# A hybrid decoder layer on one core: the sample batch's mixing and paged attention laid as strands between half units of the input projection

## The reference

```python
h = rms_norm(x, norm_g)
z = h @ w_in          # 1024 -> 5280 columns: q_r k_r v_r g_r | c_q c_kv k_pe | g_m | mg_r mg_m
# branch A: retention, 4 heads of 128, chunks of 128; rotary q and k, per-head decay, a state per head
ret = head_rms(inner + cross) * silu(g_r)
# branch B: latent attention, 8 heads; q = rms_norm(c_q) @ w_uq; keys and values from rms_norm(c_kv)
mla = softmax(q k^T * 96 ** -0.5) v * silu(g_m)
merged = sigmoid(mg_r) * (ret @ w_branch_ret) + sigmoid(mg_m) * (mla @ w_branch_mla)
y = rms_norm(x + merged @ w_out, final_gain)
```

## Time and profile before

| | |
|---|---|
| median of 3 runs | 2914.07 us (2908.35 to 2914.93) |
| profiled execution | 2911.8 us, span 2909.6 us, mean granted clock 0.926 |
| busy, share of the span | PE 2595.7 us (89%), PEld 2343.4 (81%), DVE 1365.3 (47%), ACT 1083.7 (37%), POOL 541.0 (19%) |
| DMA | 326.22 MB, mean 112 GB/s |

### The profile page before, as it was taken

The page is one execution under the profiler, slowest core; times in us unless marked ns, Lnnn a source line. Parts: engine busy times, 40 slices in busy tenths (PEclk is TensorE's granted clock), DMA queues, the critical chain, the costliest instruction groups (busy, mean ns, idle before and its releaser), DMA issues. The chain is left out here.

```text
span 2909.6 us, 46992 instructions
## 1 busy us (share of the span) xinstructions
PE 2595.7 (89%) x15975; PEld 2343.4 (81%) x15975; DVE 1365.3 (47%) x2631; ACT 1083.7 (37%) x2340; POOL 541.0 (19%) x435
## 2 busy tenths in 40 slices
PE   7899999997899999983479999498989995899998
PEld 6799999996688888862368887487878884799897
DVE  4243334444243344424256664286868884322221
ACT  3122223333122223321157776275757774211110
POOL 0000024331011034421024445000000000223230
PEclk9999999999999999996589997599999997999997
DMA  4354565552345565622244440523232303443440
GB/s 129 111 153 135 143 168 137 136 143 89 108 146 148 148 176 152 158 75 74 82 118 118 122 128 2 130 59 74 59 74 59 74 1 139 151 153 115 144 129 24
DMA packets 422336, 326.22 MB, mean 112 GB/s; under 512 B 81153, under 2 KB 391522, under 8 KB 419042
## 3 DMA queue, kind: packets, MB, share of 16 engines
q1 hardware_dynamic: 405906, 307.72, 38.1%
q10 hardware_dynamic: 16208, 15.74, 1.8%
HBM read 221.92 MB, written 101.43 MB: 111 GB/s over the span
## 5 line engine op out<-in xcount | busy, mean ns | idle before, releaser
L66 PE MATMUL f_bank<-a_h_hi,a_w_hi 128*128 128x384 f32 (+3 forms) x1680 | 609.2, 363 | 15.1 <-DVE a_zo L805 10.2
L68 PE MATMUL f_bank<-a_h_hi,a_w_lo 128*128 128x384 f32 (+3 forms) x1680 | 595.0, 354 | 0.0
L67 PE MATMUL f_bank<-a_h_lo,a_w_hi 128*128 128x384 f32 (+3 forms) x1680 | 594.6, 354 | 0.0
L66 PEld LDWEIGHTS f_bank<-a_h_hi,a_w_hi 128*128 128x128 f32 (+1 forms) x1680 | 315.3, 188 | 42.1 <-issue 15.4
L68 PEld LDWEIGHTS f_bank<-a_h_hi,a_w_lo 128*128 128x128 f32 (+1 forms) x1680 | 314.5, 187 | 30.7
L67 PEld LDWEIGHTS f_bank<-a_h_lo,a_w_hi 128*128 128x128 f32 (+1 forms) x1680 | 315.4, 188 | 26.3
L2343 DVE TENSOR_TENSOR t_pt<-t_bank,t_pt 128x512 fp32r<-128x512 f32 (+3 forms) x320 | 194.7, 609 | 68.7 <-ACT t_pt L2295 66.1
L2295 ACT ACTIVATE t_pt<-t_bank 128x512 fp32r<-128x512 f32 (+3 forms) x320 | 170.9, 535 | 140.4 <-PE t_bank L2428 139.8
L2353 DVE TENSOR_REDUCE t_mx<-t_bank 128x1 f32<-128x512 f32 (+3 forms) x320 | 192.4, 604 | 51.5 <-PE t_bank L2420 42.9
L2308 ACT ACTIVATE t_prob<-t_bank,t_nm 128x512 f32<-128x512 f32 (+3 forms) x320 | 196.7, 626 | 36.3 <-DVE t_nm L2360 35.2
L2439 PE MATMUL t_bank<-t_pt,t_vt 128*128 128x256 f32 x1088 | 192.1, 301 | 7.8 <-DVE t_pt L2343 6.3
(11 more groups left out here) (375 smaller groups left out, 5424.2 us busy)
## 6 DMA issues: line engine op xcount, KB each, us to landing
a_w_raw<-in_w_in SPq DMA_DIRECT2D x82, 512.0 KB, 4.4
p_lat<-in_lat_pool SPq DMA_DIRECT2D x208, 128.0 KB, 2.0
between_zT<-a_zo SPq DMA_DIRECT2D x82, 256.0 KB, 4.5
y_mg<-between_zT SPq DMA_DIRECT2D x128, 128.0 KB, 2.2
between_zT<-a_zo SPq DMA_DIRECT2D x82, 192.0 KB, 2.5
r_zt<-between_zT SPq DMA_DIRECT2D x16, 768.0 KB, 7.3
t_qt<-between_QT SPq DMA_DIRECT2D x16, 768.0 KB, 11.8
a_x<-in_x_prompt SPq DMA_DIRECT2D x16, 512.0 KB, 5.1
```

Of the source, the lines that this page charges most:

```text
L66: pe.matmul(out, lh, rh, start=start, stop=False)
L67: pe.matmul(out, lh, rl, start=False, stop=False)
L68: return pe.matmul(out, ll, rh, start=False, stop=stop)
```

## The change

- `mix` (for the sample rows), `latent_queries`, `attend_paged` and `latent_values` go, with their barriers. Their work becomes strands in `front`: the sample rows are tile -1 of `mla_steps(0, 8)`; then come `decode_steps()` (labels D, V), `sample_ret_steps()` (labels E), `ret_steps(0, 8)`, `mla_steps(8, 16)`, `ret_steps(8, 16)`, one chain of steps spread evenly over all of the projection from half unit 37 on.
- A group of 512 keys goes through in one sweep: each group has its own maximum, its own sum and its own values (`acc`), which `d_join` weighs together at the end of a sequence. The two parts of the rotary keys stand one above the other (64 rows), so that one matmul of 512 columns takes the place of eight of 128; the new keys are one group of 64 columns with a mask. All pages are loaded by SP, three groups ahead.
- Of the wait at a strand's start only SP's is left (and one of POOL's).
- Sigmoid becomes Tanh of half the argument in `front`: silu is (tanh + 1) z, made in `a_zo`, and the factors of 2 go into the head norm's constants and into `w_mla` and `w_out` (0.5). The scale of the scores goes into the norm of c_q; in `attend` one negated maximum replaces a maximum and a multiplication. The rotary turns have other forms of about the same size.
- The x tiles of the first half have a buffer each and are loaded at once.

In the cut below `d_load` and the branches of `which` are SP's, `d_exp` to `d_part` ACT's, the other `d_` functions PE's.

```diff
+def decode_steps():
+    out = [PAD, PAD, ("S", "D", 0), *(("DL", j) for j in range(3)), PAD, PAD, PAD, ("DN", 0), ("DT", 0), PAD]
+    late = []
+    for i in range(N_GROUPS):
+        b, g = divmod(i, PER)
+        for x in (("DS", i), ("DT", i + 1), ("DP", i), ("DO", i)):
+            out.append(x if x[1] < N_GROUPS else PAD)
+            if x[0] == "DS" and i:
+                out.append(("DN", i))
+            if late:
+                out.append(late.pop(0))
+        if g < NGD and b * NGD + g + 3 < DEC_B * NGD:
+            out.append(("DL", b * NGD + g + 3))
+        if g == NGD:
+            late += [("DE", b, k) for k in range(5)] + [("DF", b)]
+    for x in late:
+        out += [x, PAD]
+    return out + [("S", "V", 0), ("VL", 0), PAD, PAD, ("VX", 0), PAD, PAD, ("VP", 0), ("VP", 1), PAD, ("VO", 0)]
+
+def sample_ret_steps():
+    out = [PAD, PAD, ("S", "E", 0), ("EL", 0), PAD, PAD, ("Ef", 0), ("Ev", 0), ("Ef", 1), PAD, ("Eh", 0), ("Ef", 2), PAD, PAD, ("Ek", 0), ("Em", 0),
+           ("Ea", 0), PAD]
+    for h in range(RH):
+        out += [PAD, ("Eo", h), PAD, ("Es", h)]
...
 def schedule():
     (a1, b1, a2, b2), units = backbone()
...
+    first = next(i for i, x in enumerate(a1) if x[0] == "U" and x[2] == 1 and units[x[1]][0] == 6)
+    steps = mla_steps(0, 8) + decode_steps() + sample_ret_steps() + ret_steps(0, 8) + mla_steps(8, 16) + ret_steps(8, 16)
+    return a1[:first] + between(a1[first:] + b1 + a2 + b2, steps), units
...
+            def d_load(j):
+                need(sp, nl, j - 3)
+                need(sp, tq, 3 * (j - 3))
+                for k in range(4):
+                    page = sp.value_load(table[0:1, 4 * j + k:4 * j + k + 1])
+                    sp.dma_start(lat[:, j % 4, k], T["lat_pool"][ds(page, 1)].rearrange("a p c -> (a p) c")).then_inc(lin[j % 4], 16)
+                    sp.dma_start(pe[:, j % 4, k], T["pe_pool"][ds(page, 1)].rearrange("a p c -> (a p) c")).then_inc(lin[j % 4], 16)
...
+                elif which == "D":
+                    mla_over(sp, 8)
...
+                elif which == "E":
+                    sp.wait_ge(v_st, 32)
...
+                elif x[0] == "DT":
+                    if n:
+                        d_exp(n - 1)
+                    d_keys_high(n)
+                elif x[0] == "DS":
+                    d_low(n)
...
+                elif x[0] == "DP":
+                    d_probs_high(n)
+                elif x[0] == "DO":
+                    d_part(n)
...
+            def d_turn(i):
...
+                for c in range(KC):
+                    need(p, ltl, 3 * (j - 1) + c + 1)
+                    for k in range(4):
+                        mm = p.transpose(bk[:, 2 + c, k * PAGE:(k + 1) * PAGE], lat[:, j % 4, k, c * P:(c + 1) * P], ident[:])
+                    mm.then_inc(tq, 1)
+                need(p, ltl, 3 * j)
+                for k in range(4):
+                    mm = p.transpose(bk[0:ROPE, 4, k * PAGE:(k + 1) * PAGE], pe[:, j % 4, k], ident[:])
+                mm.then_inc(tq, 1)
+            def d_scores(i):
...
+                for c in range(KC):
+                    for x in range(2):
+                        p.matmul(bk[:, 5, 0:w], qall[:, c, bb], keys[x][:, c, 0:w], start=(c + x == 0), stop=False)
+                p.matmul(bk[:, 5, 0:w], qp[:, bb], rope[:, 0:w], start=False, stop=True).then_inc(qk, 1)
+            def d_probs(i):
+                bb, g = divmod(i, PER)
+                p.wait_ge(ex, i + 1)
...
+            def d_values(i):
+                bb, g = divmod(i, PER)
+                p.wait_ge(ptl, i + 1)
...
-            a.activation(sg[:, 0:n], bk[:, b, 0:n], ACT.Sigmoid).then_inc(sig, 1)
+            a.activation(zo[:, u % 3, 0:n], bk[:, b, 0:n], ACT.Tanh, scale=0.5).then_inc(sig if kind == "silu" else z_act, 1)
...
-    mix(nc, T, True)
-    decode(nc, T)
```

More of the change, by code:

```diff
@@ L112 @@
          + [(c * P, P, "silu") for c in range(3 * RH, 4 * RH)])
-GATES = [(GM0 + c * P, P, "silu") for c in range(NH * VD // P)] + [(MG0 + c * P, P, "sigmoid") for c in range(2 * D_MODEL // P)]
+GATES = [(GM0 + c * P, P, "silu") for c in range(NH * VD // P)] + [(MG0 + c * P, P, "tanh") for c in range(2 * D_MODEL // P)]
 BLOCKS = [(h, *b) for h in range(2) for b in PLAIN + GATES]
@@ L201, in mla_steps @@
         if n == lo:
-            out.append(("MX", lo, 2))
+            out.append(("MX", lo, "uv"))
         if n + 2 < hi:
@@ L275, in front @@
             event[x[:2]] = len(fate)
-            if BLOCKS[units[x[1]][0]][3] == "sigmoid":
+            if BLOCKS[units[x[1]][0]][3] == "tanh":
                 n_sig += 1
@@ L325, in front @@
                 pass
-            kn_hi, kn_lo = pair(of, "kn", [P, NH // 2, 2 * P])
+            with nc.sbuf_tensor("m_wt", [NOPE, NH, KL], F32) as w_t:
+                pass
+            with ExitStack() as k:
+                kn_hi, kn_lo = (k.enter_context(nc.sbuf_tensor("m_kn" + x, [P, NH // 2, 2 * P], F32R)) for x in ("_hi", "_lo"))
+            of("gap", [P, QC * NH * QD])
+            qall, qp = of("qall", [P, KC, DEC_B, P], F32R), of("qp", [2 * ROPE, DEC_B, P], F32R)
+            ltn = [of("ltn" + x, [P, KC, NS], F32R) for x in ("_hi", "_lo")]
@@ L797, in z_out @@
                 j, g, half_, c0, width, kind, t0, n = unit(u)
-                if kind == "sigmoid":
+                if kind == "tanh":
                     return
@@ new lines, in d_fold, with v_heads @@
+            def d_fold(bb):
+                p.wait_ge(de, 15 * (bb + 1))
+                p.wait_ge(oc, min(PER * (bb + 1) + 1, N_GROUPS))
+                for c in range(KC):
+                    mm = p.matmul(bk[:, 6, c * NS:(c + 1) * NS], tot[:, c * P:(c + 1) * P], fold[:], start=True, stop=True)
+                mm.then_inc(of_d, 1)
+            def v_heads(k):
+                p.wait_ge(v_lo_d, 2)
+                for h in range(4 * k, 4 * k + 4):
+                    f = slice(h // 2 * P, (h // 2 + 1) * P)
+                    for c in range(KC):
+                        mm = three(p, bk[:, 5, h * NS:(h + 1) * NS], uvv_hi[:, c, f], uvv_lo[:, c, f], ol_hi[:, c, h], ol_lo[:, c, h], c == 0, c == KC - 1)
+                if k:
+                    mm.then_inc(v_mm, 1)
@@ new lines, in e_outs @@
+            def e_outs(h):
+                p.wait_ge(e_a, 4)
+                p.wait_ge(e_v, 3)
+                p.wait_ge(e_qm, h + 1)
+                p.wait_ge(e_split, 2 * h + 2)
+                out = bk[0:NS, 6, h * RD:(h + 1) * RD]
+                three(p, out, ea_hi[:, h], ea_lo[:, h], ev_hi[:, h], ev_lo[:, h], True, False)
+                for b in range(DEC_B):
+                    i = three(p, out, qm[0][:, b], qm[1][:, b], es_hi[:, b], es_lo[:, b], False, b == DEC_B - 1)
+                i.then_inc(e_o, 1)
```

1865 lines of the change are left out of this document (721 added, 1144 removed).

## The result

The changed kernel takes 2962.4 us (median of four runs, 2961.4 to 2964.3) against 2914.1 us: ratio 1.016, 95% interval 1.0138 to 1.0183. It is slower by 1.6%; the forecast was 2786 us, 4.4% faster. Its profiled execution has a span of 2959.5 us, 1.9 us under its own time.

What follows compares the result with a forecast made beforehand. PE was nearly gapless in the projection but idle in the stages before `attend`. Span 2909.6 - 538.1 + 293.6 = 2665, + 56 + 78 - 15 = 2784, 2.2 more as a time: 2786 us; range 2690 to 2862.

Steps and rivals of the forecast that it cites:

- the step on the clock: At strand starts in `front`: waits of about 8 us and more cost clock, three new ones at 3.3 us each, 10 us.
- What goes, and the PE work that comes: Four stages and barriers go, 538.1 us; their work returns between half units as 293.6 us of PE time.
- Waits inside a group: In the key groups, mainly the values' product awaiting split probabilities: 0.5 us a group, 32 us, plus 24 at sequence ends, 56.
- Rival 2: Order binds: ACT's queue puts next keys before probabilities; 2 us more a group or SP's pages add 70 us: 2857; chance 0.2.
- SP's pages: SP's page loads take 6 us of a group's 9.2, with stores of z behind them; nothing was taken for it.
- Waits at strand starts: In `front`, a new strand's first step waits for its load; with denser strands and clock, 78 us in sum.
- the second half's x tiles: In the projection, 8 of the 18.4 us of waits for `a_h_lo` were to go, since group steps lie between.
- Rival 3: Slower: two table loads a key group if Exp and Tanh need different tables, 320 us, a time near 3100; chance 0.05.
- The group term's upper bound: In the key groups: 2.5 us a group, 160 us, if every probabilities' turn and values' product waits for its own chain.
- signs that were to prove the forecast wrong: PE waiting over 1.5 us a group, waits for pages or `a_zo`, or table loads beside the gates.
- signs that were to confirm it: `attend` starting near 1718 us; in the paged strand groups 9.8 us apart, PE over 90% busy at full clock.
- rival 1: All group chains hidden, leaving only strand starts: 2665 + 50 - 15, time about 2700; chance 0.2.

Runs made afterwards that it cites:

- e3: On the changed kernel, all steps of the key groups made blank slots, so the paged attention is left out; 2531.5 us.
- e2: On the changed kernel, each key group's values product done one group late, everything computed; 2891.2 us, ratio to the kernel before 0.991.
- e7: On top of e2, no strand's steps beside the 12 half units in which the second half of x is turned; 2877.5 us.
- e4: No part of the block: runs of 512-column matmuls with waits of about 0.5 to 9 us between, single and in trains; no kernel time given.
- e11: e4 again, with waits of about 1.3 to 4.4 us, each six times, behind runs of 90 to 105 matmuls; no kernel time given.
- e14: On the changed kernel, DVE makes the low half of the split probabilities three times over, lengthening each group's chain; 3044.4 us.
- e1: On the changed kernel, the groups' values product reads a static tile, so PE never waits for the split probabilities; output not attention; 2903.1 us.
- e13: On top of e2: e7's cleared half units, blank slots where strands start, two more in each retention tile; 2855.9 us, ratio to the kernel before 0.979.

## Why the prediction was wrong

The mechanism of the waits was seen, their size was not, and the step on the clock failed. The 180 us by which `front` came late are 72 of clock, 64 of idle time and 44 of dearer work.

**What goes, and the PE work that comes.** Right in kind. The groups' turns, keys and values cost more than 3.90 us: by the starts in the changed kernel at full clock DO takes 1.05 us (540.29 to 541.34) and DS 1.46, against 1.01 and 1.14. The fifth product of DS, with 64 rows, was counted at 0.227 and takes 0.43 to the next start. Some 0.3 us x 64 is about 20 us of the miss. The rest is for the most part what a change of kind costs on either side of a step: in a half unit of 384 columns the first product behind a DS, DT or DP takes 0.26 to 0.28 us to the next start in place of 0.173, and the one ahead of a DP 0.27. By an estimate of three such places a group that is another 20 us; where the few us that are left lie is open. The sum priced every product as if its like stood beside it.

```profile
541.34 0.40 PE L1595 MATMUL f_bank<-d_lt_hi,m_qall 128*128 128x512 f32 x1
...
542.37 0.50 PE L1596 MATMUL f_bank<-d_rt,m_qp 64*128 64x512 f32 x1
542.80 0.44 PE L66 MATMUL f_bank<-a_h_hi,a_w_hi 128*128 128x384 f32 x1
543.08 0.34 PE L67 MATMUL f_bank<-a_h_lo,a_w_hi 128*128 128x384 f32 x1
543.26 0.33 PE L68 MATMUL f_bank<-a_h_hi,a_w_lo 128*128 128x384 f32 x1
```

**Waits inside a group.** The place was named, DO for its probabilities, and so was the reason, no half unit in one pair of three. The size was not: 104 us by e3, less 11.6 for the first pages, against 56, with 58.7 for `d_pt` alone where 32 stood. Rival 2 had half of the mechanism: ACT's in-order queue, with the next keys ahead of this group's probabilities. DVE's queue holds them up as much. One of the waits, from the timelines of PE, ACT and DVE:

```profile
610.32 0.46 PE L1605 MATMUL f_bank<-a_ident,d_prob 64*128 64x64 f32 x4
610.74 0.57 ACT L982 ACTIVATE d_rt<-f_bank 32x512 fp32r<-32x512 f32 x1
611.22 0.36 ACT L1003 ACTIVATE d_pt<-f_bank 128x256 fp32r<-128x256 f32 x1
610.40 1.29 DVE L1164 TENSOR_TENSOR d_lt_lo<-f_bank,d_lt_hi 128x512 fp32r<-128x512 f32 x2 [1.50 <-ACT d_lt_hi L980]
611.72 0.68 DVE L1164 TENSOR_TENSOR d_rt<-f_bank,d_rt 32x512 fp32r<-32x512 f32 x1
612.43 0.42 DVE L1164 TENSOR_TENSOR d_pt<-f_bank,d_pt 128x256 fp32r<-128x256 f32 x1
612.91 0.39 PE L1615 MATMUL f_bank<-d_nat_hi,d_pt 128*128 128x256 f32 x1 [2.13 <-DVE d_pt L1164]
```

ACT copies the turned probabilities at 611.22, behind the rotary keys, and DVE splits them at 612.43, behind its own work on the same keys. Summed over all waits for `d_pt`, ACT came to the probabilities some 24 us after they were turned, and DVE some 35 us after ACT's copy. Where both are free the wait is 0.93 us, and it was counted at 1. e2, which changes only the order, takes the waits away. But by itself rival 2 gave 2857 and not 2962. SP's pages held nothing up: only the first, 11.6 us.

**Waits at strand starts.** Nearly right: without the groups `front` stands 137.8 us (e3) where 109 were counted, and the difference is about what the retention waits for `r_a_lo`. The first pages, forecast 11, waited 11.6; `e_zg` and the states 17.7 for 21. The retention's 24.6 us were missed: its strands were costed at their starts only. And the second half's x tiles, which were to gain 8 us beside the groups, lost: 31.5 us for `a_h_lo` against 18.4; e7 gets 9 us of waits back.

**The step that failed: "A wait of about 8 us and more also costs clock ... Three such new waits, 3.3 us each: 10."** It was drawn from the one window of the earlier trace rows, where the wait was long, and nothing bounded it for short ones, though the change was about to make dozens. The trace of the kernel before could have bounded it: there the clock was also at 0.50 behind a wait of 4.85 us for `a_zo` and at one of 3.04 us for `a_h_lo`.

```profile
400.60:407.40 6.80, 4.80 (x15) 4.83 (x16) 2.18 (x3) 1.77 (x3) 2.57 (x2) 0.50 0.43 138
704.40:707.80 3.40, 3.05 (x10) 2.60 (x11) 0.89 (x2) 0.60 (x1) 0.00 (x0) 0.50 0.00 0
```

For a long wait the price of 3.3 us was even too high: of the 10.2 us at 0.50 around the wait in the earlier trace rows PE is busy in 3.3, so 1.7 were lost. What failed is the bound of 8 us, with many shorter waits under it. PE's busy time at 1.2 GHz rose from 21 to 185 us, and half of the difference, 82 us, is work lost; 10 were in the sum. So of the 180 us by which `front` came late 72 are this step. e4, e11 and e14 show with bare matmuls and in the kernel that waits of some 2 us and more do this; e1 shows the limit, since waits of 1.4 us cost little beside themselves. Of the 93 us lost 10 lie ahead of the groups, 37 beside them and 45 behind them, where the retention is. How much of these is due to waits and how much to small products, as at 156.6 us, stays open, and so does why the retention's chain is short of time: e13 shows that spacing helps, not which queue is behind.

**The rivals.** Rival 3, table loads, did not come: one in the whole kernel, none beside Exp and Tanh, as the Trainium skill ("ScalarE: Activation LUTs", "Table sets: the hidden batching unit") has it for sets that hold both.

```profile
L875 ACT ACT_TABLE_LOAD x1 | 1.3, 1283 | 7.6 <-DMA a_x<-in_x_prompt 7.6
```

Slower came all the same, by a way that none of the cases held: rival 2's waits, and the clock behind them and behind the others. The group term's upper bound, 2.5 us, multiplied waits but never the speed of the work behind them. None of the signs that were to prove the forecast wrong came: PE's waits in the groups are about 1.3 us a group and not over 1.5, none over 4.3 us but the one for the first pages, and no table load stands beside the gates. What failed were signs that were to confirm it: groups 11.7 us apart for 9.8, PE busy 86% of their stretch for over 90%, a clock of 0.95, and `attend` 180 us late. No sign was set on the clock as one that would prove it wrong. Two side sums don't come out: rival 1 has 50 us for the strand starts where the sum has 78, without a working, and in rival 2 two us a group more would be 128 us, not 70.

## What to carry to other kernels

When work is laid between pieces that keep TensorE busy, count the waits it will make and not their sum alone. Between bare matmuls waits up to some 1.6 us cost only themselves here; from 2.3 to 2.9 us about one in two cost another 1.6 us, and from 4.4 us every one did, because the matmuls behind it run at 1.2 GHz while PE still reads as fully busy. In the kernel the edge is less sharp: the clock also fell at 903.9 us, at a wait of 1.53. Look at the sum of durations of work that the change doesn't touch; it tells clock loss at once. And between a product and the step that needs its copies leave one other step of its kind: one line of order (e2) was worth 71 us here, more than the whole change had lost.

## What the runs showed of the hardware

- Between bare matmuls (e4, e11) the granted clock fell to 1.2 GHz behind waits as short as 1.8 us (2 of 9), and not behind one of 69 waits up to 1.6 us. The stretch at 552.5 us lasted until 555.9, at a mean of 0.50.
- Waits of equal length did not act alike: at 3.38 us none of three in e4 and six of six in e11.
- The clock also fell without a wait: it was 0.50 from 156.6 to 163.4 us of the changed kernel with PE busy all the time, behind 48 products of 64 rows and 64 columns.
- In DS of the changed kernel the product of 512 columns over 64 rows took PE 0.43 us to the start of the next step's, the last one over 128 rows 0.33, the others 0.23 to 0.24. The first product of 384 columns behind it took 0.28 where its neighbours take 0.17.
